# Begin of the value product in a product-key expert layer: order of row gathers, cell gathers and prepared activations, and the dense spill in two tensors

## The chip, the cores and the metric

The kernel runs on one core of one Trainium2 chip. The metric is the device time of one launch in microseconds (us). Three runs of the kernel before gave 3905.82, 3908.99 and 3909.05 us, median 3908.99 us.

## The reference

A decoder trunk of two layers, one sequence of 512 tokens, width 1024, all in float32. The part that this change touches is the retrieval of experts:

```
def peer_ffn(xn, w_query, sub_keys, expert_u, expert_v):
    q = einsum('bsd,dn->bsn', xn, w_query).reshape(b, s, 8, 2, 128)
    scores = einsum('bshpc,hpkc->bshpk', q, sub_keys)
    half_vals, half_idx = top_k(scores, 16)
    ...                                    # 256 sums per head, top 16 of them
    gates = softmax(top_vals)              # 8 heads x 16 = 128 slots per token
    u = take(expert_u, i_t)                # 16384 experts
    act = gelu(einsum('ted,td->te', u, x_t)) * g_t
    return einsum('te,ted->td', act, take(expert_v, i_t))
```

Before it in each layer stand the input projection, stick-breaking attention, a short convolution, a pooling mixer, gates and an output projection; behind it a gated embedding of the layer (`w_ple_gate`, `w_ple_proj`).

## The kernel before, in words

The host lays all weights out as one stream of tiles of 128 x 1024 float32 (512 KB), and the kernel works through them one by one. Each tile goes the same way: the SP queue loads it into one of 4 `raw` buffers (line 328), ScalarE rounds it to `hi` (`split`, line 453), VectorE or GpSimd takes the rest `lo = raw - hi` (`split`, lines 775 and 401), and TensorE multiplies with three products, hi x high, hi x low and lo x high. There are 8 buffers of `hi` and `lo` (`RING`), and tiles are split four ahead of their use (`AHEAD`). A `raw` buffer is loaded again as soon as `lo` of its tile is taken.

**The dense stage (U).** All 16384 experts are 128 tiles of `expert_u`. `experts` multiplies each tile with all 512 tokens (24 matmuls of 512 columns, line 1218). ScalarE takes the gelu into `eo` (`dense_gelu`, line 604) and spills its row of 512 tokens to the DRAM tensor `early`, of shape 128 x 128 x 512, by one DMA on its own queue (line 607), 256 KB each. `early_out` counts these DMAs. Meanwhile the softmax gates of the first 384 tokens (`M`) are scattered into `gate_table`.

**The value stage (V).** It treats two kinds of tokens apart, side by side.

- The first 384 tokens (`M` = 3 blocks of 128) go through all 128 tiles of `expert_v`. Four tiles are a group (`EG` = 4, `NG` = 32 groups per layer). For a group, ScalarE fetches gates `gb` and activations `eb` (`fetch`, lines 652 and 655, 768 KB each), VectorE multiplies them into `af` (`gated`, line 1115), ScalarE rounds to `ah` (`high`, line 660), VectorE takes `al = af - ah` (`low`, line 1122). TensorE then runs `values` (line 1434): 4 tiles x 3 blocks x 3 products x 2 halves = 72 matmuls of 512 columns. It waits for `al_ready` at the start of the group and for `lo_split` ahead of each tile. The sums stay in six PSUM banks.
- The last 128 tokens are not multiplied densely. Each has 128 slots, a slot being one chosen expert. For slot q of all 128 tokens, GpSimd gathers one activation each, the *cells* (`cells(q)`, line 413, an indirect DMA into column q of `hval`), and one row of `expert_v` each, the *rows* (`rows(j)`, line 421, an indirect DMA of 512 KB into one of 4 buffers `vrow`). VectorE multiplies four columns of cells with their gates into `aval` (line 1132) and adds `vrow * aval` to `acc` (the *axpy*, line 1137).

VectorE does one `period` per group. Its order is fixed: `gated` of the next group, wait for the four cells of this group (`h_in`, two semaphores in turn), `aval`, then four times a wait for a row, an axpy and a `split`, with `low` of the next group behind the second split. So a VectorE that waits for cells holds back the splits and `low` behind them. `low` of group g + 1 stands in the period of group g.

GpSimd's order before is written out: it waits for the last spill, issues cells 0 to 3, and then in turn `rows(j)`, `cells(j + 4)`. `rows(j)` from j = 4 on waits until the axpy of row j - 4 is done:

```
for q in range(4):
    cells(q)
for j in range(SLOTS):
    rows(j)
    if j + 4 < SLOTS:
        cells(j + 4)
```

At the end of V the sums of the 384 tokens and `acc` are turned back and added to `hT`.

## Time and profile before

| | us |
|---|---|
| median of three runs | 3908.99 |
| time of the profiled execution | 3910.81 |
| its span (first to last instruction) | 3909.0 |
| PE busy, share of the span | 3828.8, 98% |
| DVE busy, share | 2878.5, 74% |
| POOL busy, share | 1474.3, 38% |
| ACT busy, share | 1450.8, 37% |
| mean DMA rate over the span | 189 GB/s |
| mean granted TensorE clock | 0.992 of full speed |

The engines are PE (TensorE matmuls), DVE (VectorE), ACT (ScalarE), POOL (GpSimd) and SP (the load queue). A row of the timeline gives start, duration, engine, line and operation, and in square brackets how long the engine had been idle and what ended that. A q behind an engine's name is its DMA queue: for it, busy is the time of issuing. The chain of waits is the one sequence of work that ended last. "issue" as a releaser means that the profile shows nothing waited for.

### The profile page before, as it was taken

Reading aid. Unit: us, or ns where it says so; the run is one execution under the profiler, and the core shown is the slowest. Engines: PE = TensorE matmul, PEld = TensorE weight load, DVE = VectorE, ACT = ScalarE, POOL = GpSimd, SP = SyncE. Lnnn points to the kernel's source line nnn. Section 1 sums busy time; section 2 is a strip of 40 time slices with the busy share of each in tenths; the row PEclk is TensorE's granted clock in tenths of the full one; section 3 lists DMA queues with packets and bytes.
Section 4 is the critical chain, followed back from the end, with each engine's and each line's share of the span. In section 5 each row is a group of like instructions: output and inputs, shape, how many; then the busy total and the mean of one; then the engine's idle time right before and its main releaser. Section 6 shows DMA issues by size and latency. Waiting matters only on the chain.

```text
span 3909.0 us, 53929 instructions
## 1 busy us (share of the span) xinstructions
PE 3828.8 (98%) x17258; PEld 3140.4 (80%) x17258; DVE 2878.5 (74%) x4061; ACT 1450.8 (37%) x1957; POOL 1474.3 (38%) x935
## 2 busy tenths in 40 slices
PE   8999999999999999999999999999999999999997
PEld 5777888888888878888767778888888887888886
DVE  6753658989997287788577536599899963888785
ACT  5533333333333333333444333333333333333334
POOL 1100003444444277666101000045444443777651
PEclk9999999999999999999999999999999999999998
DMA  3222223445554699999222223234455546999991
GB/s 114 70 86 97 92 92 123 144 172 189 187 188 175 209 357 360 358 352 342 102 69 77 85 93 101 88 131 145 172 194 192 189 165 231 370 361 352 351 330 70
DMA packets 323770, 740.36 MB, mean 189 GB/s; under 512 B 30497, under 2 KB 161697, under 8 KB 319905
## 3 DMA queue, kind: packets, MB, share of 16 engines
q1 hardware_dynamic: 104400, 381.73, 28.1%
q10 hardware_dynamic: 174160, 222.40, 16.6%
q0 software_dynamic: 45056, 134.38, 9.3%
q8 instruction: 72, 1.18, 0.1%
q14 instruction: 82, 0.66, 0.1%
HBM read 618.87 MB, written 119.54 MB: 189 GB/s over the span
## 4 chain that ended last, share of the span: by engine, by line
PE 95%; DVE 2%; issue 1%; ACT 1%; DMA 1%; POOL 0%; DVEq 0%; ACTq 0%; POOLq 0%; SPq 0%
PE banks L1218 62%; PE banks L1434 26%; PE banks L1413 2%; PE banks L1280 1%; PE banks L1270 1%; PE banks L1288 1%; PE banks L1360 0%; ACT hi L453 0%; PE banks L1265 0%; DVE xl L787 0%; DMA vrow<-in_stream,tail_v 0%; DVE lo L775 0%; DMA raw<-in_stream 0%; ACT xh L469 0%; DVE xl L956 0%
## 5 line engine op out<-in xcount | busy, mean ns | idle before, releaser
L1218 PE MATMUL banks<-xh,hi 128*128 128x512 f32 x3264 | 1293.1, 396 | 27.1 <-DVE xl L787 18.5
L1218 PE MATMUL banks<-xl,hi 128*128 128x512 f32 x3264 | 1276.0, 391 | 0.0
L1218 PE MATMUL banks<-xh,lo 128*128 128x512 f32 x3264 | 1273.7, 390 | 0.0
L401 POOL TENSOR_TENSOR lo<-raw,hi 128x1024 fp32r<-128x1024 f32 x240 | 646.0, 2692 | 984.0 <-ACT hi L453 983.8
L775 DVE TENSOR_TENSOR lo<-raw,hi 128x1024 fp32r<-128x1024 f32 x484 | 586.6, 1212 | 418.2 <-ACT hi L453 351.7
L453 ACT ACTIVATE hi<-raw 128x1024 fp32r<-128x1024 f32 x724 | 739.5, 1042 | 261.3 <-DMA raw<-in_stream 162.6
L1218 PEld LDWEIGHTS banks<-xh,hi 128*128 128x128 f32 x3264 | 615.4, 189 | 166.0 <-DVE xl L787 23.6
L1218 PEld LDWEIGHTS banks<-xh,lo 128*128 128x128 f32 x3264 | 614.6, 188 | 130.9
L1218 PEld LDWEIGHTS banks<-xl,hi 128*128 128x128 f32 x3264 | 616.0, 189 | 122.4 <-issue 5.6
L1434 PE MATMUL banks<-hi,ah 128*128 128x512 f32 x1536 | 475.2, 391 | 13.2 <-issue 11.7
L1434 PE MATMUL banks<-lo,ah 128*128 128x512 f32 x1536 | 474.4, 390 | 0.0
L1434 PE MATMUL banks<-hi,al 128*128 128x512 f32 x1536 | 473.8, 390 | 0.0
L604 ACT ACTIVATE eo<-banks 128x512 f32<-128x512 f32 x256 | 153.3, 599 | 838.5 <-PE banks L1218 815.7
L413 POOL DMA_INDIRECT hval<-early,tail_h x256 | 395.7, 1546 | 167.1 <-DMA early<-eo 86.2
L1072 DVE TENSOR_TENSOR LB<-found,gates 128x1024 fp32r<-128x1024 f32 x192 | 414.1, 2157 | 0.1
L421 POOL DMA_INDIRECT vrow<-in_stream,tail_v x256 | 318.8, 1245 | 216.9 <-DVE acc L1137 145.7
L1137 DVE SCALAR_TENSOR_TENSOR acc<-vrow,aval,acc 128x1024 f32<-128x1024 f32 x256 | 330.5, 1291 | 43.5 <-DMA vrow<-in_stream,tail_v 24.2
L1434 PEld LDWEIGHTS banks<-hi,ah 128*128 128x128 f32 x1536 | 289.0, 188 | 74.8 <-issue 14.9
L1434 PEld LDWEIGHTS banks<-lo,ah 128*128 128x128 f32 x1536 | 289.4, 188 | 60.3
L1434 PEld LDWEIGHTS banks<-hi,al 128*128 128x128 f32 x1536 | 289.1, 188 | 60.3
L1066 DVE TENSOR_TENSOR found<-iota,tabs 128x1024 fp32r<-128x1024 f32 x192 | 233.6, 1217 | 42.7 <-PE banks L1413 42.7
L660 ACT ACTIVATE ah<-af 128x1536 fp32r<-128x1536 f32 x64 | 95.4, 1491 | 430.9 <-issue 209.7
(211 smaller groups left out, 3442.0 us busy)
## 6 DMA issues: line engine op xcount, KB each, us to landing
raw<-in_stream SPq DMA_DIRECT2D x724, 512.0 KB
early<-eo ACTq DMA_DIRECT2D x256, 256.0 KB, 2.4
gate_table<-stage ACTq DMA_DIRECT2D x24, 2048.0 KB, 7.1
gb<-gate_table ACTq DMA_DIRECT2D x64, 768.0 KB
eb<-early ACTq DMA_DIRECT2D x64, 768.0 KB
hval<-early,tail_h POOLq DMA_INDIRECT x256
vrow<-in_stream,tail_v POOLq DMA_INDIRECT x256
hT<-in_xT ACTq DMA_DIRECT2D x2, 1024.0 KB, 8.1
```

The lines of the kernel that those rows point to most:

```text
L401: pool.tensor_tensor(lo[k % RING][:, :], raw[k % RAW][:, :], hi[k % RING][:, :].bitcast(f32), ALU.subtract).then_inc(lo_split, 1)
L413: pool.indirect_dma_start(hval[:, q:q + 1], None, early_cells, bass.IndirectOffsetOnAxis(tail_h[:, q:q + 1], 0)).then_inc(h_in[q // 4 % 2] ...
L421: pool.indirect_dma_start(vrow[j % 4][:, :], None, stream_rows, bass.IndirectOffsetOnAxis(tail_v[:, j:j + 1], 0)).then_inc(vrow_in[j % 4], 16)
L453: act.activation(hi[k % RING][:, 0:w], raw[k % RAW][:, 0:w], ACT.Copy).then_inc(hi_split, 1)
L604: act.activation(eo[:, k % 2, :], bank[4 + k % 2][:, :], ACT.Gelu_apprx_tanh).then_inc(act_evac, 1)
L660: act.activation(ah[:, u, :, :], af[:, :, :], ACT.Copy).then_inc(ah_ready, 1)
L775: dve.tensor_tensor(lo[k % RING][:, 0:w], raw[k % RAW][:, 0:w], hi[k % RING][:, 0:w].bitcast(f32), ALU.subtract).then_inc(lo_split, 1)
L1066: dve.tensor_tensor(found[:, u, :, :, :], iota[:, :].unsqueeze(1).unsqueeze(1).to_broadcast(two), tabs[:, 0:2, cut].unsqueeze(3).to_broadc ...
L1072: dve.tensor_tensor(LB[:, u, :, :, :], found[:, u, 0, :, :].bitcast(f32).unsqueeze(2).to_broadcast(four), gates[:, :, cut].bitcast(f32).re ...
L1137: dve.scalar_tensor_tensor(acc[:, :], vrow[r][:, :], aval[:, z, r:r + 1], acc[:, :], ALU.mult, ALU.add).then_inc(axpy_done, 1)
L1218: ins = pe.matmul(out_ap, st[slot][:, a:a + P], mv, start=first and i == 0, stop=last and i == 2)
L1434: ins = pe.matmul(bank[m * 2 + h][:, :], a[:, z, k, m * P:(m + 1) * P], w[s % RING][:, h * SEQ:(h + 1) * SEQ], start=first and k == 0 and ...
```

## The change

Four edits.

1. GpSimd issues rows 0 to 3 first, ahead of the wait for the last spill and of all cells. Then cells 0 to 3, and from then on `cells(j)`, `rows(j)` with the same j.
2. VectorE's first two periods of V are written out of the loop. The first (`opens`) does `gated(1)`, the first split, `low(1)` and `gated(2)` and only then waits for the cells; no split stands behind its first axpy. The second (`taken`) leaves out its `gated`. The loop over the rest has one trip fewer. `Steps.loop` gets a start.
3. The dense spill goes to two tensors: `early`, now 128 x 128 x 384, for the first 384 tokens, and `late`, 128 x 128 x 128, for the others. That is two DMAs per tile in place of one (192 and 64 KB), and the counts of `early_out` are doubled.
4. `eb` is fetched from `early` without gaps: 4 x 384 values in one piece for each partition. The cells are gathered from `late`, with the indices worked out for it.

```diff
     @contextmanager
-    def loop(self, trips, per):
+    def loop(self, trips, per, start=0):
         base, k = self.base, self.k
-        with self.eng.Fori(0, trips) as i:
-            self.base, self.k = i * per + (base + k), 0
+        with self.eng.Fori(start, start + trips) as i:
+            self.base, self.k = i * per + (base + k - start * per), 0
...
-    early = nc.dram_tensor("early", (P, NK, SEQ), f32, kind="Internal").ap()
-    early_cells = early.rearrange("p e (t o) -> (p e t) o", o=1)
+    early = nc.dram_tensor("early", (P, NK, M), f32, kind="Internal").ap()
+    late = nc.dram_tensor("late", (P, NK, P), f32, kind="Internal").ap()
+    late_cells = late.rearrange("p e (t o) -> (p e t) o", o=1)
...
                 pool.wait_ge(tail_ready, l + 1)
                 pool.wait_ge(tile_done, RING + l * T + N_V)
+                for j in range(4):
+                    rows(j)
                 for u in range(2):
-                    pool.wait_ge(early_out[u], 16 + (l + 1) * (NK * 8))
+                    pool.wait_ge(early_out[u], 32 + (l + 1) * (NK * 16))
                 for q in range(4):
                     cells(q)
-                for j in range(SLOTS):
+                for j in range(4, SLOTS):
+                    cells(j)
                     rows(j)
-                    if j + 4 < SLOTS:
-                        cells(j + 4)
...
-                    act.dma_start(early[:, bass.ds(row, 1), :].rearrange("p a t -> p (a t)"), eo[:, k % 2, :])\
+                    act.dma_start(early[:, bass.ds(row, 1), :].rearrange("p a t -> p (a t)"), eo[:, k % 2, 0:M])\
+                       .then_inc(early_out[k % 2], 16)
+                    act.dma_start(late[:, bass.ds(row, 1), :].rearrange("p a t -> p (a t)"), eo[:, k % 2, M:SEQ])\
                        .then_inc(early_out[k % 2], 16)
...
-                    act.dma_start(eb[:, u, :, :], early[:, bass.ds(g * EG, EG), 0:M]).then_inc(early_in[u], 16)
+                    act.dma_start(eb[:, u, :, :], early[:, bass.ds(g * EG, EG), :]).then_inc(early_in[u], 16)
...
-                def period(i, z, prep=True):
+                def begin(g, u, turn):
+                    dve.wait_ge(al_ready, l * NG + g)
+                    gated(g, u, turn)
+                def period(i, z, prep=True, opens=False, taken=False):
                     k0 = N_V + z * EG + AHEAD
-                    if prep:
-                        dve.wait_ge(al_ready, l * NG + i * 2 + z + 1)
-                        gated(i * 2 + z + 1, 1 - z, i + (1 + z))
+                    g = i * 2 + z + 1
+                    if prep and not taken:
+                        begin(g, 1 - z, i + (1 + z))
+                    if opens:
+                        split(l, k0, i)
+                        low(g, 1 - z)
+                        begin(g + 1, z, i + (1 + z))
                     dve.wait_ge(h_in[z], l * (SLOTS * 8) + i * 64 + 64)
...
-                        split(l, k0 + r, i)
-                        if prep and r == 1:
-                            low(i * 2 + z + 1, 1 - z)
+                        if not opens or r > 0:
+                            split(l, k0 + r, i)
+                        if prep and r == 1 and not opens:
+                            low(g, 1 - z)
...
-                with steps.loop(NG // 2 - 1, DVE_TURN) as i:
+                period(0, 0, opens=True)
+                period(0, 1, taken=True)
+                with steps.loop(NG // 2 - 2, DVE_TURN, 1) as i:
                     period(i, 0)
                     period(i, 1)
```

GpSimd at the begin of V, before. `hval` are the cells, `vrow` the rows.

```order
L413 DMA hval<-early,tail_h 128x1 [waits early_out0,early_out1]
L413 DMA hval<-early,tail_h 128x1 x3
L421 DMA vrow_178<-in_stream,tail_v 128x1024
L413 DMA hval<-early,tail_h 128x1
L421 DMA vrow_179<-in_stream,tail_v 128x1024
L413 DMA hval<-early,tail_h 128x1
L421 DMA vrow_180<-in_stream,tail_v 128x1024
L413 DMA hval<-early,tail_h 128x1
L421 DMA vrow_181<-in_stream,tail_v 128x1024
L413 DMA hval<-early,tail_h 128x1
L419 ISA
L421 DMA vrow_178<-in_stream,tail_v 128x1024 [waits axpy_done]
```

Eight cells stand ahead of the first row that waits for an axpy (row 4): the cells of groups 0 and 1.

The same place after the change:

```order
L422 DMA vrow_179<-in_stream,tail_v 128x1024
L422 DMA vrow_180<-in_stream,tail_v 128x1024
L422 DMA vrow_181<-in_stream,tail_v 128x1024
L430 ISA
L414 DMA hval<-late,tail_h 128x1 [waits early_out0,early_out1]
L414 DMA hval<-late,tail_h 128x1 x4
L420 ISA
L422 DMA vrow_178<-in_stream,tail_v 128x1024 [waits axpy_done]
L414 DMA hval<-late,tail_h 128x1
L420 REGISTER_ALU
L422 DMA vrow_179<-in_stream,tail_v 128x1024 [waits axpy_done]
L414 DMA hval<-late,tail_h 128x1
```

Rows 0 to 3 have moved to the front, and five cells stand ahead of the first waiting row; cells 5, 6 and 7 now stand behind rows 4, 5 and 6, each of which waits for an axpy. In the rest of V the last cell of each group of four stands in the same way behind the third row of that group.

VectorE at the begin of V after the change (before, `aval` came directly behind the first `af`):

```order
L1119 TENSOR_TENSOR af<-eb,gb 128x1536
L778 REGISTER_ALU
L779 TENSOR_TENSOR lo_73<-raw_61,hi_65 128x1024
L1125 REGISTER_ALU
L1126 TENSOR_TENSOR al<-af,ah 128x1536
L1119 TENSOR_TENSOR af<-eb,gb 128x1536
L1144 ISA
L1145 TENSOR_TENSOR aval<-hval,tail_g 128x4
```

A split, `low(1)` and `gated(2)` have moved ahead of `aval`, which is the first instruction that needs cells.

## Rows read from the trace of the kernel before

**Rows 1.** Page, part 1: busy us (share of the span) and instructions by engine.

```profile
PE 3828.8 (98%) x17258; PEld 3140.4 (80%) x17258; DVE 2878.5 (74%) x4061; ACT 1450.8 (37%) x1957; POOL 1474.3 (38%) x935
```

**Rows 2.** What PE waited for: us in total, times, longest.

```profile
PE banks L1434 <- issue: 11.7, 2, 6.2
```

**Rows 3.** Timeline of PE at V's begin, both layers (start, us, what).

```profile
1353.13 0.72 PE L1434 MATMUL banks<-hi,ah 128*128 128x512 f32 x2 [0.76 <-ACT eo L604]
...
1369.14 0.61 PE L1434 MATMUL banks<-hi,al 128*128 128x512 f32 x2
1375.24 1.22 PE L1434 MATMUL banks<-hi,ah 128*128 128x512 f32 x2 [5.49 <-issue]
...
1380.18 0.62 PE L1434 MATMUL banks<-hi,ah 128*128 128x512 f32 x2
...
3314.41 1.22 PE L1434 MATMUL banks<-hi,ah 128*128 128x512 f32 x2 [6.23 <-issue]
...
3318.71 0.62 PE L1434 MATMUL banks<-hi,al 128*128 128x512 f32 x2
```

**Rows 4.** Chain of waits, in order of time: start, us, what.

```profile
1375.24 508.33 PE banks L1434 x2232
```

**Rows 5.** Timeline of POOL at V's begin.

```profile
1356.03 1.15 POOL L413 DMA_INDIRECT hval<-early,tail_h  x1 [43.13 <-DMA early<-eo]
...
1361.05 0.94 POOL L413 DMA_INDIRECT hval<-early,tail_h  x1 [0.31 <-issue]
1362.29 0.94 POOL L421 DMA_INDIRECT vrow<-in_stream,tail_v  x1 [0.30 <-issue]
```

**Rows 6.** Timeline of DVE at V's begin.

```profile
1356.91 1.76 DVE L1115 TENSOR_TENSOR af<-eb,gb 128x1536 f32<-128x1536 f32 x1 [0.64 <-DVE acc L1153]
1367.03 0.16 DVE L1132 TENSOR_TENSOR aval<-hval,tail_g 128x4 f32 x1 [8.36 <-DMA hval<-early,tail_h]
1368.64 1.28 DVE L1137 SCALAR_TENSOR_TENSOR acc<-vrow,aval,acc 128x1024 f32<-128x1024 f32 x1 [1.45 <-DMA vrow<-in_stream,tail_v]
```

**Rows 7.** Timeline of DVE in the second period of V: cells, `low`, the last axpy.

```profile
1381.46 0.15 DVE L1132 TENSOR_TENSOR aval<-hval,tail_g 128x4 f32 x1
...
1386.54 1.75 DVE L1122 TENSOR_TENSOR al<-af,ah 128x1536 fp32r<-128x1536 f32 x1
...
1393.10 1.32 DVE L1137 SCALAR_TENSOR_TENSOR acc<-vrow,aval,acc 128x1024 f32<-128x1024 f32 x1 [2.43 <-DMA vrow<-in_stream,tail_v]
```

**Rows 8.** Timeline of POOL beside it: rows 7 and 10, then a cell.

```profile
1382.66 1.27 POOL L421 DMA_INDIRECT vrow<-in_stream,tail_v  x1 [0.31 <-issue]
...
1391.91 0.94 POOL L421 DMA_INDIRECT vrow<-in_stream,tail_v  x1 [0.30 <-issue]
1393.16 0.94 POOL L413 DMA_INDIRECT hval<-early,tail_h  x1 [0.31 <-issue]
```

**Rows 9.** Timeline of POOL in the middle of V: a cell behind a waiting row.

```profile
1618.92 3.72 POOL L413 DMA_INDIRECT hval<-early,tail_h  x1 [0.30 <-issue]
```

**Rows 10.** Stretches: PE, PEld, DVE, ACT, POOL busy, PEclk, DMA share, GB/s.

```profile
1360.00:1368.00 8.00, 8.00 (x37) 6.60 (x36) 0.16 (x1) 3.14 (x4) 6.17 (x7) 1.00 0.99 306
1400.00:1860.00 460.00, 460.00 (x2031) 380.91 (x2030) 371.19 (x316) 157.50 (x145) 318.71 (x227) 1.00 0.99 354
```

**Rows 11.** DMA queues (packets, MB, share of 16 engines), and the spill's issues.

```profile
q1 hardware_dynamic: 104400, 381.73, 28.1%
q10 hardware_dynamic: 174160, 222.40, 16.6%
...
early<-eo ACTq DMA_DIRECT2D x256, 256.0 KB, 2.4
```

**Rows 12.** Timeline of ACT: the last gelu of the first layer's dense stage.

```profile
1352.40 0.60 ACT L604 ACTIVATE eo<-banks 128x512 f32<-128x512 f32 x1 [3.81 <-PE banks L1218]
...
1353.03 0.34 ACTq L607 DMA_DIRECT2D early<-eo  x1
```

**Rows 13.** Timeline of DVE: the last axpy of the first layer.

```profile
1868.35 1.28 DVE L1137 SCALAR_TENSOR_TENSOR acc<-vrow,aval,acc 128x1024 f32<-128x1024 f32 x1
```

14 lines of the change are left out of this document (7 added, 7 removed).

## The prediction, made before the change had run

> **What bounds the kernel now.** I read the busy shares first: TensorE is at 98% of the span, and the next engine, VectorE, at 74% [rows 1]. So only what TensorE waits for is worth anything, and the second view is that list. In the value stage it has one kind of entry, 11.7 us in two waits [rows 2], one for each layer. The third view is its place. TensorE starts group 0 of V at 1353.13; the last pair of matmuls of that group starts at 1369.14, a pair takes 0.45 us, and the next one starts only at 1375.24 [rows 3]. That is 5.65 us of standing still. Then TensorE runs at half speed: the six pairs up to 1380.18 take 4.94 us, where 2.72 would do, 2.2 us more. So the begin of V costs 7.9 us in the first layer, and 6.4 + 2.0 = 8.4 us in the second (idle 6.23 us, then five pairs in 4.30 us) [rows 3]. From there TensorE runs 2232 matmuls, which is 31 groups, in 508.33 us without a wait [rows 4]; less the 2.2 us that is **16.33 us for a group**.
>
> Why it stood: VectorE waited 8.36 us for the first four cells, until 1367.03 [rows 6], and `low(1)` and the splits for group 1 stand behind that wait. The cells were late because GpSimd could issue them only from 1356.03, when the last spill had landed [rows 5]; the fourth was issued by 1361.99 and landed, with VectorE's start, at 1367.03. So **a cell takes 5.04 us from the end of its issue to its use**.
>
> **The change, part by part.**
>
> *The begin.* `gated(1)`, the first split, `low(1)` and `gated(2)` now stand ahead of the wait for cells. `gated(1)` ended at 1358.67 before [rows 6]; with one split and one `low` behind it `al` of group 1 is there by about 1362, well ahead of 1369.6. GpSimd issues its four rows from about 1352.5, when the dense stage has ended, then cells 0 to 3. Four cells took 5.96 us before, and an issue repeats every 1.25 us at best [rows 5], so four rows end by 1358.5, four cells by 1363.5, and the cells are used at 1363.5 + 5.04 = 1368.5. Two axpys and a split later, about 4.0 us, the second tile of group 1 is split at 1372.6; TensorE wants it at 1369.6 + 4.1 = 1373.7. **The wait at group 1 goes: 7.9 and 8.4 us, 16.3 us in all.**
>
> *The order of the cells.* What is late next is the last cell of each later group. Before, eight cells stood ahead of the first row that waits; a cell was always issued four slots ahead of its own row. Now cell 4p + 3 is issued behind row 4p + 2, which waits for the axpy of row 4p - 2. This axpy is the third of the period before, and VectorE has only a split, an axpy, a split and `gated` between it and the wait for that cell. This makes a ring: cells used, three axpys, two splits and `low`, row issued, cell issued, cell landed, cells used. I price it from the second period, where VectorE ran from `aval` to the third axpy without a pause. `aval` is at 1381.46, `low` ends at 1388.29, the row behind the third axpy is issued at 1391.91 and the cell behind it by 1394.10 [rows 7, 8]. That is 12.64 us, and with the landing 12.64 + 5.04 = **17.68 us a group**, over the 16.33 that TensorE needs. From then on TensorE waits for `low` in every group.
>
> The landing is the unknown, since no row shows a cell that is waited for in the middle of V. From below: the spill, a DMA of another queue, lands 2.4 us after issue [rows 11]. From above: row 7 was issued by 1383.93 and used only at 1393.10 after a wait of 2.43 us, 9.17 us [rows 7, 8], with the DMA engines full. I take 5.04, the only row that shows the operation itself; it was measured with a DMA share of 0.99, and V now runs at 0.99 and 354 GB/s [rows 10]. At 17.68 us a group the same bytes would make 327 GB/s, close to the 306 beside those cells.
>
> For this landing a rule stands against the row. The Trainium skill, page "DMA: Bandwidth & Descriptors", section on the anatomy of one DMA, gives a DMA issued by GpSimd about 2.0 us and its bytes on top, so some 2 us for a cell. By it a group would take 14.6 us, below TensorE's 16.33, and nothing would be lost. The same page, section on queues, rings and completion order, says that a completion is written only after every earlier write of that DMA engine, across its queues. By that a cell ends no earlier than the rows and loads ahead of it, and the 5.04 us agree.
>
> *The sum, first layer.* Before cells 4 to 7 are complete, GpSimd issues row 4 (0.8 us behind the first axpy, at 1370.9), cell 5, row 5, cell 6, row 6 and cell 7, six issues at 1.25 us, to about 1378.1. They are used at 1383.1, and `low(2)` ends 6.83 us later at 1389.9, where TensorE wanted it at 1385.9: the wait has moved by one group. 29 further groups of 17.68 us lead to `low(31)` at 1902.7, and one group of matmuls to 1919.0. Before, V ended at 1375.24 + 508.33 = 1883.6 [rows 4]. That is 35.4 us more, already with the begin's gain in it; the second layer, whose begin gave 0.5 us more away, 34.9. Together 70.3 us: 3981.1 for the profiled execution's 3910.8, and since the median of the runs lies 1.8 us below that, **3979 us**.
>
> *The spill in two pieces.* 256 more issues on ScalarE's queue at 0.34 us [rows 12] are 87 us of issuing, at nothing: ScalarE is idle for 3.8 us of each tile [rows 12]. Without that cover they would be the 87 us. The pieces land 2.4 us after issue and are wanted again two tiles later, 48 matmuls of 0.227 us or 10.9 us. At V's begin the second piece lands some 0.4 us later than the one before did, behind GpSimd's four rows. Nothing.
>
> *`eb` without gaps.* The ACT queue, with the small pieces, took 16.6% for 222 MB, the load queue, with pieces of 4 KB, 28.1% for 382 MB [rows 11]: 0.075 and 0.074% for a MB. So larger pieces give the DMA engines next to nothing back; between 0 and perhaps 0.2 us of a landing. The trip written out of VectorE's loop adds instructions that are fetched once: nothing, up to a us a layer.
>
> *The end of V.* The last axpy ended at 1869.63 [rows 13], 14 us ahead of TensorE. In the ring that lead shrinks to about a us behind `low(31)` plus one group; the turning back waits for it only after 2.7 us of other matmuls. Nothing, at most 2 us a layer.
>
> **The rivals.**
>
> *The cell lands soon enough (faster).* The point from which it decides is a landing of 3.69 us, where the ring is as long as TensorE's group. For it: the rule above; the spill's 2.4 us; and that GpSimd's pace in the priced period was partly its own backlog, so that the ring may be a us or so shorter. Against it: 5.04, measured, and rows at over 5 us. With a landing of 2.4 us, cells 4 to 7 are used at 1380.5, `low(2)` ends 1.4 us late, and the rest runs at 16.33: 6.4 and 7.0 us gained, 3910.8 - 13.4, for the median **3896 us**. If even this 1.4 us is hidden, 3893. Chance 0.27.
>
> *The ring is as long as TensorE's group.* Break even is where 29 groups give back the begin, a group of 16.47 us: 3909 us. Chance 0.06.
>
> *The ring is longer still.* For it: the cell behind a waiting row took 3.72 us to issue in the middle of V [rows 9], 2.8 more than the one I priced. With one cell in three like that, a group takes 18.6 us and the kernel about 4033 us; with all of them 20.5 and about 4140; with the row's 9.17 us of landing 21.8 and about 4230. Against it: as a group gets longer the DMA engines have less to do. I count it within the slower case, which has 0.67; a tenth lies beyond 4055.
>
> *The begin gains nothing.* If the rows ahead make the first cells land later than 1369.5, TensorE waits at the second tile of group 1. It would cost up to what was saved, 16 us, and changes no sign; it lies within the range of the slower case.
>
> **How the numbers follow.** A measurement of this kernel tells about 0.2%, 8 us, from no change. Slower 0.67, the same 0.06, faster 0.27. In the slower case alone the time goes from 3927 us (a cell lands together with the row ahead of it: the first row took 5.4 us from 1363.23 to its axpy at 1368.64 [rows 5, 6], less 1.25 us, a group of 16.8) to 4055 (18.9 a group). The range must reach the faster case, so 3892 to 4055.
>
> **What would show it.** In the trace of the changed kernel: no wait of TensorE at group 1; TensorE waiting in V not once but at nearly every group, by 1 to 1.5 us each; VectorE's `aval` with a wait for cells of 2 us or more in each period; a distance of 17 to 18.5 us from `aval` to `aval`; V longer by 35 us a layer; GpSimd's cells evenly behind its rows. I am wrong if `aval` waits for less than a us in the middle of V and TensorE runs without gaps there. Then the landing was the term that failed, and V is about 6 to 8 us shorter a layer.

## The result, and the profile after

| | us |
|---|---|
| before, median of 6 runs | 3909.88 (3905.82 to 3911.20) |
| after, median of 6 runs | 4182.64 (4156.32 to 4192.57) |
| ratio, 95% interval | 1.0685 (1.0648 to 1.0722) |
| profiled execution after: time, span | 4156.32, 4154.5 |
| mean granted TensorE clock, before and after | 0.992, 0.969 |

The change makes the kernel 273 us slower. The forecast said slower, 3979 us, with a range to 4055: the sign came, the size did not. Where the runs of one program below lie more than 1.5% apart, the ratio is that of the faster ones alone.

The page of the kernel after, parts 1, 4 and 5. A group's row gives busy us and mean ns of one, then the idle time before it and what ended most of it.

```profile
PE 3913.9 (94%) x17258; PEld 3188.2 (77%) x17258; DVE 2858.3 (69%) x4061; ACT 1466.9 (35%) x1957; POOL 1532.7 (37%) x935
...
PE 65%; issue 15%; DMA 11%; DVE 4%; POOL 4%; ACT 1%; DVEq 0%; POOLq 0%; ACTq 0%; SPq 0%
...
L414 POOL DMA_INDIRECT hval<-late,tail_h x256 | 376.0, 1469 | 78.0 <-issue 78.0
...
L1145 DVE TENSOR_TENSOR aval<-hval,tail_g 128x4 f32 (+1 forms) x64 | 10.4, 163 | 451.3 <-DMA hval<-late,tail_h 451.3
```

What PE waited for, after: us in total, times, longest.

```profile
PE banks L1450 <- DVE al L1126: 159.8, 45, 6.9
...
PE banks L1234 <- DVE lo L779: 9.3, 2, 5.7
...
PE banks L1450 <- DVE lo L779: 1.9, 2, 1.1
```

(L1234 with `lo` is the first multiplication behind V; the other two are in V.) Where V knew two waits of 11.7 us in all [rows 2], TensorE now waits 45 times for `al`, 159.8 us. The cells have come into the chain that ended last (`hval`, in the 11% of DMA), and VectorE stands 451.3 us for them in 64 periods. The account closes: the waits above make 171.0 us, 159.3 more than the 11.7 before. PE's busy time, for the same 17258 matmuls, went from 3828.8 [rows 1] to 3913.9, 85.1 more. Together that is 244.4 of the 245.5 us by which the span grew. The busy part is matmuls at half speed behind the waits. It is no loss of its own where VectorE sets the pace: there the slow matmuls only fill a part of the stop, as the groups below show.

**The begin of V.** Timeline of PE, first layer:

```profile
1375.55 0.73 PE L1450 MATMUL banks<-hi,ah 128*128 128x512 f32 x2 [1.05 <-DVE lo L779]
...
1394.29 1.22 PE L1450 MATMUL banks<-hi,ah 128*128 128x512 f32 x2 [6.18 <-DVE al L1126]
```

Timeline of VectorE there:

```profile
1371.35 0.16 DVE L1145 TENSOR_TENSOR aval<-hval,tail_g 128x4 f32<-128x4 f32 x1 [7.28 <-DMA hval<-late,tail_h]
...
1387.26 0.16 DVE L1145 TENSOR_TENSOR aval<-hval,tail_g 128x4 f32<-128x4 f32 x1 [7.00 <-DMA hval<-late,tail_h]
...
1392.35 1.74 DVE L1126 TENSOR_TENSOR al<-af,ah 128x1536 fp32r<-128x1536 f32 x1
```

Timeline of POOL there:

```profile
1354.00 1.14 POOL L422 DMA_INDIRECT vrow<-in_stream,tail_v  x1 [40.44 <-PE banks L1234]
...
1361.33 1.76 POOL L414 DMA_INDIRECT hval<-late,tail_h  x1 [0.30 <-issue]
1363.40 1.49 POOL L414 DMA_INDIRECT hval<-late,tail_h  x1 [0.31 <-issue]
...
1373.85 1.32 POOL L422 DMA_INDIRECT vrow<-in_stream,tail_v  x1 [6.46 <-DVE acc L1150]
...
1381.50 0.95 POOL L414 DMA_INDIRECT hval<-late,tail_h  x1 [0.31 <-issue]
```

The wait at group 1 (5.49 us [rows 3]) is down to 1.05. At group 2 there is one of 6.18, and behind it the first pair takes 1.22 us, the half speed. The first cells are used at 1371.35; they had been priced at 1368.5. GpSimd began 1.5 us later than priced, and three of its issues took 1.5 to 1.8 us instead of 0.94.

**The middle of V** has two kinds of groups. The distance from `aval` to `aval` is about 17.8 us in one and about 21.7 in the other (medians). Over the first layer it is 20.30 on average (from 1371.35 to 2000.53 in 31 steps). A short one, VectorE:

```profile
1405.07 0.16 DVE L1145 TENSOR_TENSOR aval<-hval,tail_g 128x4 f32 x1 [4.54 <-DMA hval<-late,tail_h]
...
1410.55 1.75 DVE L1126 TENSOR_TENSOR al<-af,ah 128x1536 fp32r<-128x1536 f32 x1
...
1413.42 1.26 DVE L779 TENSOR_TENSOR lo<-raw,hi 128x1024 fp32r<-128x1024 f32 x1
1414.61 1.32 DVE L1150 SCALAR_TENSOR_TENSOR acc<-vrow,aval,acc 128x1024 f32<-128x1024 f32 x1
1415.85 1.21 DVE L779 TENSOR_TENSOR lo<-raw,hi 128x1024 fp32r<-128x1024 f32 x1
...
1423.29 0.16 DVE L1145 TENSOR_TENSOR aval<-hval,tail_g 128x4 f32 x1 [4.56 <-DMA hval<-late,tail_h]
```

The same, GpSimd: a row, the third cell of the four, the row behind it, and the last cell.

```profile
1411.76 1.36 POOL L422 DMA_INDIRECT vrow<-in_stream,tail_v  x1 [0.30 <-issue]
1413.43 0.94 POOL L414 DMA_INDIRECT hval<-late,tail_h  x1 [0.30 <-issue]
1414.67 0.95 POOL L422 DMA_INDIRECT vrow<-in_stream,tail_v  x1 [0.30 <-issue]
1415.93 1.96 POOL L414 DMA_INDIRECT hval<-late,tail_h  x1 [0.30 <-issue]
```

A long one, VectorE:

```profile
1713.89 0.17 DVE L1145 TENSOR_TENSOR aval<-hval,tail_g 128x4 f32 x1 [8.44 <-DMA hval<-late,tail_h]
...
1721.80 1.22 DVE L779 TENSOR_TENSOR lo<-raw,hi 128x1024 fp32r<-128x1024 f32 x1
1722.93 1.28 DVE L1150 SCALAR_TENSOR_TENSOR acc<-vrow,aval,acc 128x1024 f32<-128x1024 f32 x1
1724.13 1.22 DVE L779 TENSOR_TENSOR lo<-raw,hi 128x1024 fp32r<-128x1024 f32 x1
1725.26 1.75 DVE L1119 TENSOR_TENSOR af<-eb,gb 128x1536 f32<-128x1536 f32 x1
1735.48 0.16 DVE L1145 TENSOR_TENSOR aval<-hval,tail_g 128x4 f32 x1 [8.47 <-DMA hval<-late,tail_h]
```

The same, GpSimd:

```profile
1721.81 2.03 POOL L414 DMA_INDIRECT hval<-late,tail_h  x1 [0.30 <-issue]
1724.14 3.69 POOL L422 DMA_INDIRECT vrow<-in_stream,tail_v  x1 [0.31 <-issue]
1728.13 0.95 POOL L414 DMA_INDIRECT hval<-late,tail_h  x1 [0.30 <-issue]
```

And TensorE behind it:

```profile
1738.48 0.61 PE L1450 MATMUL banks<-hi,al 128*128 128x512 f32 x2
1742.59 1.22 PE L1450 MATMUL banks<-hi,ah 128*128 128x512 f32 x2 [3.49 <-DVE al L1126]
...
1745.91 0.63 PE L1450 MATMUL banks<-lo,ah 128*128 128x512 f32 x2
```

In both kinds the third cell meets the third split of the period, to a hundredth of a us. That is no chance: the row ahead of it is held by `low` and ends 0.82 us after `low` does (1411.76 + 1.36 = 1413.12, and 1410.55 + 1.75 = 1412.30), 0.30 us pass between two issues, and the third split begins 1.12 us behind `low` too (1413.42), with one axpy between them.

In the short group the cell starts 0.01 us behind the split, takes 0.94, and the row behind it finds only an axpy. In the long one it starts 0.01 us behind the split as well, yet takes 2.03: it ends at 1723.84, 0.82 us after the split's end (1723.02). Now the row begins level with the fourth split, which `gated` follows without a gap, and ends at 1727.83, again 0.82 us after the end of `gated` (1727.01). The last cell is issued 15.19 us after `aval` (1729.08 less 1713.89), in the short group 12.82 (1417.89 less 1405.07). It lands after 6.40 us instead of 5.40.

Of the 60 groups behind the first of each layer, the row took over 3 us in 34. In these the last cell was issued 15.3 us after `aval` on average and landed in 6.2, in the others 13.2 and 5.4. I call the third cell held when its issue takes over 1.9 us; of the 56 cells for which the trace has the cell and the split beside it, 36 were held.

TensorE follows: behind a stop of 3.49 us it goes at half speed, four pairs up to 1745.91 take 3.32 us where 1.81 would do. The 21.59 us of this group are TensorE's 16.33, these 1.5 and the stop of 3.5 (21.3). At full speed the stop would have been 1.5 us longer and the group as long.

### The profile page after: what moved, and what is told of

The parts are those of the page before. It is cut to its first block, busy times and chain, and to the rows that moved or that the text cites. A ratio compares the mean times of both kernels' runs of the same rounds, so it can differ in the third digit from the quotient of the medians.

```text
span 4154.5 us, 54167 instructions
## 1 busy us (share of the span) xinstructions
PE 3913.9 (94%) x17258; PEld 3188.2 (77%) x17258; DVE 2858.3 (69%) x4061; ACT 1466.9 (35%) x1957; POOL 1532.7 (37%) x935
## 3 DMA queue, kind: packets, MB, share of 16 engines
q10 hardware_dynamic: 186448, 222.42, 15.7%
## 4 chain that ended last, share of the span: by engine, by line
PE 65%; issue 15%; DMA 11%; DVE 4%; POOL 4%; ACT 1%; DVEq 0%; POOLq 0%; ACTq 0%; SPq 0%
PE banks L1234 59%; DMA hval<-late,tail_h 11%; POOL vrow L422 3%; DVE acc L1150 2%; PE banks L1429 2%; PE banks L1296 1%; PE banks L1286 1%; PE banks L1304 1%; POOL hval L414 1%; PE banks L1376 0%; ACT hi L455 0%; PE banks L1281 0%; DVE xl L791 0%; DVE aval L1145 0%; DVE lo L779 0%
## 5 line engine op out<-in xcount | busy, mean ns | idle before, releaser
L1234 PE MATMUL banks<-xh,hi 128*128 128x512 f32 x3264 | 1293.2, 396 | 27.9 <-DVE xl L791 19.3
L1234 PE MATMUL banks<-xl,hi 128*128 128x512 f32 x3264 | 1276.4, 391 | 0.0
L1234 PE MATMUL banks<-xh,lo 128*128 128x512 f32 x3264 | 1273.8, 390 | 0.0
L1234 PEld LDWEIGHTS banks<-xh,hi 128*128 128x128 f32 x3264 | 615.6, 189 | 166.5 <-DVE xl L791 24.4
L1234 PEld LDWEIGHTS banks<-xh,lo 128*128 128x128 f32 x3264 | 614.9, 188 | 130.8
L1234 PEld LDWEIGHTS banks<-xl,hi 128*128 128x128 f32 x3264 | 616.1, 189 | 122.8 <-issue 5.6
L1450 PE MATMUL banks<-hi,ah 128*128 128x512 f32 x1536 | 509.2, 414 | 163.4 <-DVE al L1126 159.8
L422 POOL DMA_INDIRECT vrow<-in_stream,tail_v x256 | 396.3, 1548 | 503.6 <-DVE acc L1150 352.9
L1450 PE MATMUL banks<-lo,ah 128*128 128x512 f32 x1536 | 497.7, 407 | 0.0
L1450 PE MATMUL banks<-hi,al 128*128 128x512 f32 x1536 | 495.0, 405 | 0.0
L1450 PEld LDWEIGHTS banks<-hi,ah 128*128 128x128 f32 x1536 | 303.4, 201 | 246.8 <-issue 182.3
L414 POOL DMA_INDIRECT hval<-late,tail_h x256 | 376.0, 1469 | 78.0 <-issue 78.0
L1076 DVE TENSOR_TENSOR LB<-found,gates 128x1024 fp32r<-128x1024 f32 x192 | 395.3, 2059 | 0.1
L1450 PEld LDWEIGHTS banks<-lo,ah 128*128 128x128 f32 x1536 | 305.3, 199 | 67.7
L1450 PEld LDWEIGHTS banks<-hi,al 128*128 128x128 f32 x1536 | 303.6, 198 | 66.7
L1145 DVE TENSOR_TENSOR aval<-hval,tail_g 128x4 f32 (+1 forms) x64 | 10.4, 163 | 451.3 <-DMA hval<-late,tail_h 451.3
## 6 DMA issues: line engine op xcount, KB each, us to landing
eb<-early ACTq DMA_DIRECT2D x64, 768.0 KB, 10.7
```

What stands on the lines that cost most here:

```text
L414: pool.indirect_dma_start(hval[:, q:q + 1], None, late_cells, bass.IndirectOffsetOnAxis(tail_h[:, q:q + 1], 0)).then_inc(h_in[q // 4 % 2], 16)
L422: pool.indirect_dma_start(vrow[j % 4][:, :], None, stream_rows, bass.IndirectOffsetOnAxis(tail_v[:, j:j + 1], 0)).then_inc(vrow_in[j % 4], 16)
L1076: dve.tensor_tensor(LB[:, u, :, :, :], found[:, u, 0, :, :].bitcast(f32).unsqueeze(2).to_broadcast(four), gates[:, :, cut].bitcast(f32).re ...
L1234: ins = pe.matmul(out_ap, st[slot][:, a:a + P], mv, start=first and i == 0, stop=last and i == 2)
L1450: ins = pe.matmul(bank[m * 2 + h][:, :], a[:, z, k, m * P:(m + 1) * P], w[s % RING][:, h * SEQ:(h + 1) * SEQ], start=first and k == 0 and ...
```

## The experiments

**e1, the spill alone.** Edits 3 and 4, in the kernel before:

```diff
-    early = nc.dram_tensor("early", (P, NK, SEQ), f32, kind="Internal").ap()
+    early = nc.dram_tensor("early", (P, NK, M), f32, kind="Internal").ap()
+    late = nc.dram_tensor("late", (P, NK, P), f32, kind="Internal").ap()
...
+                    act.dma_start(late[:, bass.ds(row, 1), :].rearrange("p a t -> p (a t)"), eo[:, k % 2, M:SEQ])\
```

> The kernel before with the spill alone changed: two DMAs per tile, `early` without gaps, cells gathered from `late`. Theory (a ring: the last cell of a group stands behind a row that waits for an axpy): the ring is not there, so 3909 us within 6 us, and no wait for cells in the middle of V. Rival (gathering from `late`, or the small pieces, makes a cell land later and that is what costs): 4100 us or more.

Measured: 3907.45 us (3906.21 to 3911.63), the kernel before beside it 3908.37; ratio 0.9998 (0.9989 to 1.0008), as expected. The 256 more issues and the pieces without gaps cost and give nothing.

**e2, GpSimd's order alone.** In the kernel before:

```diff
-                for j in range(SLOTS):
+                for j in range(4):
+                    rows(j)
+                for j in range(4, SLOTS):
+                    cells(j)
                     rows(j)
-                    if j + 4 < SLOTS:
-                        cells(j + 4)
```

(cells 0 to 3 stand ahead of all rows, as before.)

> The kernel before with GpSimd's order alone changed: cells 0 to 3 first as before, rows 0 to 3, then cells(j), rows(j). Theory of the ring: all of the loss and none of the begin's gain, so 4170 to 4210 us, and 18 to 22 us from aval to aval. Rival (the spill, or VectorE's new begin, is to blame): 3905 to 3915 us.

Measured: 4019.39 us (4009.62 to 4022.82); 1.0278 (1.0261 to 1.0295). What PE waited for in V:

```profile
PE banks L1435 <- DVE al L1123: 78.1, 47, 7.2
```

Here the ring is what the prediction had priced: 18.0 us a group on average in both layers, 12.97 and 12.84 from `aval` to the end of the last cell's issue, 5.03 and 5.12 from there to the next `aval`. Only 1 of 55 third cells was held. So the order costs 111 us, and the changed kernel loses 163 more by something that this program has not got. The expectation, written from the long groups, was wrong.

**e3, the lead of four given back** in the changed kernel (rows 0 to 3 still first):

```diff
-                for q in range(4):
+                for q in range(8):
                     cells(q)
                 for j in range(4, SLOTS):
-                    cells(j)
                     rows(j)
+                    if j + 4 < SLOTS:
+                        cells(j + 4)
```

> The changed kernel with only the cells' lead given back: cells 0 to 7, then rows(j), cells(j + 4). Theory of the ring: the loss of 270 us goes altogether, what is left is the gain at V's begin. That gain is 16.3 us less the waits that the changed kernel still shows at group 1 for the splits (9.3 us in two, with some half speed behind them): 3895 to 3905 us. Rival (spill or VectorE's begin cost): 4100 us or more.

Measured: 3900.43 us (3896.00 to 3905.90); 0.9979 (0.9969 to 0.9988). The whole loss is gone by the place of one kind of instruction: 282 us below the changed kernel, and 8 below the kernel before, which is what is left of the begin's gain. This is what had been expected.

**e4, VectorE's begin alone**, edit 2 in the kernel before:

```diff
-                    if prep:
-                        dve.wait_ge(al_ready, l * NG + i * 2 + z + 1)
-                        gated(i * 2 + z + 1, 1 - z, i + (1 + z))
+                    g = i * 2 + z + 1
+                    if prep and not taken:
+                        begin(g, 1 - z, i + (1 + z))
+                    if opens:
+                        split(l, k0, i)
+                        low(g, 1 - z)
+                        begin(g + 1, z, i + (1 + z))
...
```

> The kernel before with VectorE's begin alone changed: a split, low(1) and gated(2) ahead of the wait for cells; GpSimd's order as before. Theory: the cells are used at 1367.0 as before, the second axpy ends at about 1371.2 and the split behind it at 1372.4, ahead of TensorE's 1373.7, so the whole wait goes without any row ahead of the cells: 3892 to 3896 us. Rival (the rows must be ahead as well): TensorE waits at group 1 for the splits by 3 us or more a layer, 3900 to 3909 us.

Measured: 3905.40 us (3902.28 to 3909.95); 0.9992 (0.9982 to 1.0001). Timeline of PE:

```profile
1388.83 1.22 PE L1446 MATMUL banks<-hi,ah 128*128 128x512 f32 x2 [3.86 <-DVE al L1122]
```

The wait at group 1 is gone, and one of 3.86 us (3.76 in the second layer) stands at group 2, with slow matmuls behind it that cost 1.4 and 1.6 us. The first cells are used at 1366.30, about as before. What holds `low(2)` up is rows: ahead of it VectorE waits 2.18, 2.54, 1.26 and 1.06 us for them, and its second `aval` waits for nothing. The expectation of 3892 to 3896 us missed; the time is the rival's, but not by the rival's wait.

**e5 and e6: which edit makes the groups long.** e5 is e2 and e1 together, e6 the changed kernel without edits 3 and 4 (one tensor `early` again, the diff of e1 backwards). e5:

```diff
-                for j in range(SLOTS):
+                for j in range(4):
+                    rows(j)
+                for j in range(4, SLOTS):
+                    cells(j)
                     rows(j)
...
+    late = nc.dram_tensor("late", (P, NK, P), f32, kind="Internal").ap()
```

> The kernel before with GpSimd's order and the spill in two, without rows ahead and without VectorE's new begin. The order alone cost 111 us, the whole change 274. Theory S (the missing 163 us are the spill's, which costs nothing without the ring but lengthens the ring): 4170 to 4200 us, 20 us or more a group. Theory D (the missing part comes with rows ahead and VectorE's begin): 4010 to 4030 us, 17.9 us a group. Theory P (it is a matter of how GpSimd's issues fall against VectorE's tensor_tensor instructions, which hold them up; any shift may tip it): in between, with long and short groups in one run.

Measured: 4006.26 us (4002.19 to 4016.41); 1.0250 (1.0235 to 1.0266), 17.8 us a group, and of 56 third cells none was held. So theory S is out.

> The changed kernel with the spill as before (one DMA per tile, `early` for all tokens). Theory S: 4000 to 4030 us. Theory D: 4150 to 4200 us. Theory P: whichever, but the time goes by the number of groups in which the row ahead of the last cell takes 3.7 us to issue: some 4 us for each such group over 17.5 us.

Measured, four runs: 4083.49, 4102.18, 4182.72 and 4186.54 us; 1.0468 (1.0441 to 1.0494). In the profiled one, the longest, a group takes 20.8 and 20.5 us and 45 of 56 third cells are held. So the long groups do not need the spill. Against e5 two things are new, edit 2 and the four rows ahead of the first cells; which of them brings the long groups was not run. Neither changes anything inside the loops that run these groups. That the two shorter executions had fewer long groups was not seen, since only one was profiled; and as both lie below all six of the changed kernel, it is not shown either that the spill has no part in how many there are.

**e7, another form of the instruction.** In the changed kernel the splits and `low` of V's periods are written as one `scalar_tensor_tensor`, times 1.0, less `hi`, which is the axpy's form:

```diff
-                    dve.tensor_tensor(al[:, u, :, :], af[:, :, :], ah[:, u, :, :].bitcast(f32), ALU.subtract)\
+                    dve.scalar_tensor_tensor(al[:, u, :, :], af[:, :, :], 1.0, ah[:, u, :, :].bitcast(f32), ALU.mult, ALU.subtract)\
...
```

> The changed kernel with VectorE's splits and low in V's periods written as scalar_tensor_tensor (times 1.0, minus), which takes some 0.06 us more each and computes the same. Theory P (a tensor_tensor on VectorE holds up GpSimd's issue until 0.8 us behind its end, a scalar_tensor_tensor does not): hardly an issue over 2 us but beside gated, from aval to the end of the last cell's issue 11 to 12 us instead of 14.3, a group of about 17, 3970 to 4020 us. Rival (what holds GpSimd up is VectorE's work as such, or its own queue): nothing changes, 4150 to 4200 us.

Measured, four runs: 4066.00, 4172.41, 4198.29 and 4201.22 us. In the profiled execution (4201.22) 20.8 us a group, and issues of 2.03 and 3.69 us as before, 43 of 53 third cells held. The form is not what holds an issue up; theory P is wrong in this point.

**e8, no fetches from group 3 on**, in the changed kernel:

```diff
-                            fetch(i * 2 + z + 3, 0, 1 - z)
+                            act.sem_inc(gate_in[1 - z], 16)
+                            act.sem_inc(early_in[1 - z], 16)
```

> The changed kernel without the fetches of gates and activations from group 3 on, which leaves their 1.5 MB a group out (old contents are used). Theory (a cell lands late because bytes of other queues and the rows are ahead of it): from the end of the cell's issue to aval 4.5 us or less on the mean, where the changed kernel shows 5.8; 4080 to 4140 us. Rival (a gather's landing is a fixed time): 5.5 us or more, and the time within 1% of 4183 us.

Measured, two runs: 4007.85 and 4026.45 us; 1.0274 (1.0248 to 1.0301). Windows of 200 us in V: PE, PEld, DVE, ACT, POOL busy, PEclk, DMA share, GB/s. The changed kernel:

```profile
1700.00:1900.00 200.00, 173.63 (x694) 139.80 (x693) 121.91 (x104) 52.85 (x48) 121.41 (x77) 0.90 0.81 271
```

e8:

```profile
1700.00:1900.00 200.00, 188.78 (x800) 152.61 (x799) 143.81 (x123) 59.63 (x55) 139.43 (x89) 0.97 0.69 233
```

42 of 57 third cells are held, as in the changed kernel, and `aval` to the last issue is as long, 14.4 and 14.6 us. But the landing falls from 5.9 and 5.7 to 3.7 and 3.6 us, and a group from 20.3 and 19.9 to 18.1. The time fell further than expected. Most of it falls where the fetches are issued ahead of the last cell. In the long group above they start at 1727.19 and 1727.76, and the cell is issued by 1729.08; in the short one the cell is out by 1417.89, ahead of the fetches at 1418.91 and 1419.47. With the fetches gone the landing falls from 6.2 to 3.1 us in the groups with a long row, and only from 5.4 to 4.6 in the others. So on average 2.2 us of a landing, and 3.1 in a long group, belong to the fetches. The Trainium skill, page "DMA: Bandwidth & Descriptors", section on queues, rings and completion order, has a completion written only after every earlier write of that DMA engine; the runs are in line with it, 5.9 us with the fetches and 3.7 without, though they do not tell it from a shared rate.

**e9, a nudge.** In the changed kernel VectorE also clears one column, ahead of the third split:

```diff
+    nudge = sb("nudge", o_c + 3904, [P, 1])
...
+                        if r == 2:
+                            dve.memset(nudge[:, :], 0.0)
```

> The changed kernel with one tiny instruction more on VectorE in each period: a memset of one column ahead of the split behind the third axpy. In the traces so far GpSimd's issue of the sixth of eight (the cell behind row 4p + 5) and this split begin within 0.02 us of each other; where the issue is first or level it takes 0.94 us and the group 17.5, where it is 0.01 to 0.02 us late it takes 2.03, the row behind it 3.7 and the group 21.8. Theory (this tie decides): the added work lets GpSimd be first every time, no group over 20 us but a few at loop ends, and the kernel gets FASTER by some 170 us for doing more: 3990 to 4020 us. Rival (the long groups have another cause, as the rows ahead or the landing): 4150 to 4200 us as before.

Measured: 4009.34 us (4004.95 to 4011.36); 1.0255 (1.0241 to 1.0269). **An instruction more in each period, and the kernel is 173 us faster.** Timeline of VectorE:

```profile
1728.40 0.16 DVE L1146 TENSOR_TENSOR aval<-hval,tail_g 128x4 f32 x1 [4.48 <-DMA hval<-late,tail_h]
...
1736.43 1.25 DVE L780 TENSOR_TENSOR lo<-raw,hi 128x1024 fp32r<-128x1024 f32 x1
1736.45 0.06 DVE L1154 MEMSET nudge<- 128x1 f32 x1
...
1746.28 0.16 DVE L1146 TENSOR_TENSOR aval<-hval,tail_g 128x4 f32 x1 [4.55 <-DMA hval<-late,tail_h]
```

GpSimd:

```profile
1736.43 0.94 POOL L415 DMA_INDIRECT hval<-late,tail_h  x1 [0.30 <-issue]
1737.67 0.94 POOL L423 DMA_INDIRECT vrow<-in_stream,tail_v  x1 [0.30 <-issue]
1738.92 1.96 POOL L415 DMA_INDIRECT hval<-late,tail_h  x1 [0.30 <-issue]
```

TensorE, and the same window as above:

```profile
1735.44 0.73 PE L1453 MATMUL banks<-hi,ah 128*128 128x512 f32 x2 [1.14 <-DVE al L1127]
```

```profile
1700.00:1900.00 200.00, 189.23 (x814) 153.26 (x815) 148.59 (x139) 61.88 (x56) 122.12 (x92) 0.99 0.93 318
```

(The program has the memset ahead of the split, the profile 0.02 us behind its start: at this grain its order is not to be trusted.) Of 57 third cells none is held; 55 start level with the split or 0.01 us ahead, 2 start 0.01 us behind. A group takes 17.8 and 17.7 us, 12.5 and 5.2 in its two parts. TensorE stands 1.1 us instead of 3.5, starts at full speed, and the granted clock in this window is 0.99 instead of 0.90. The forecast from the tie came true in sign and size, with nothing else changed: the long groups hang on it.

**e10, a lead of two** in the changed kernel:

```diff
-                for q in range(4):
+                for q in range(6):
                     cells(q)
                 for j in range(4, SLOTS):
-                    cells(j)
                     rows(j)
+                    if j + 2 < SLOTS:
+                        cells(j + 2)
```

> The changed kernel with the cells two slots ahead of their rows in place of level (cells 0 to 5, then rows(j), cells(j + 2)). The last cell of a group then stands behind row 4p + 5, which the second axpy releases, not the third: issued some 3 to 5 us sooner in the ring. Theory: from aval to the end of the last cell's issue 9 to 10 us, a ring of 14 to 16 us, under TensorE's 16.33, so all of the loss goes: 3898 to 3912 us. Rival (the lead of four is needed, for a landing of 9 us as the rows show): 3930 us or more.

Measured: 3907.90 us (3903.12 to 3910.20); 0.9996 (0.9987 to 1.0006). The last cell is now issued 9.0 and 9.1 us after `aval`, and `aval` follows 6.7 and 6.6 us later: 15.7 us on average, below TensorE's 16.33. In 5 of the 31 steps of the first layer `aval` did not wait for cells at all, so not all of the 6.7 is landing. The loss ends there. Against e3, 7.5 us are missing; stops and slow matmuls at the begin make 9.0 us in both layers where e3 has 4.6. PE's waits in the first layer:

```profile
1375.48 0.74 PE L1451 MATMUL banks<-hi,ah 128*128 128x512 f32 x2 [1.56 <-DVE lo L780]
...
1390.54 0.72 PE L1451 MATMUL banks<-hi,ah 128*128 128x512 f32 x2 [2.49 <-DVE al L1127]
```

**e11 and e12: all four splits ahead of the first cells.** e11 is e3 with this, e12 is e4 with it (cells first):

```diff
+                        for r in range(1, 4):
+                            split(l, k0 + r, i)
...
-                        if not opens or r > 0:
+                        if not opens:
                             split(l, k0 + r, i)
```

> Candidate for the best version: the kernel with the cells' lead of four given back, and in VectorE's first period all four splits ahead of the wait for cells. The kernel with the lead alone (3900.4 us) still showed waits of 2.4 and 0.8 us at group 1 for the splits and 1.0 and 0.3 at group 3. Theory: the first pair goes, with the half speed behind it: 3893 to 3898 us. Rival (the splits free raw buffers, their four loads lie ahead of the cells in the DMA engines, and low(2) comes late instead): 3900 to 3910 us with a wait of TensorE at group 2.

Measured: 3900.70 us (3898.35 to 3904.22); 0.9979 (0.9970 to 0.9988). Timeline of PE:

```profile
1388.18 0.72 PE L1453 MATMUL banks<-hi,ah 128*128 128x512 f32 x2 [2.45 <-DVE al L1127]
```

> The other candidate: the kernel before, with GpSimd's order and spill untouched, and VectorE's new begin with all four splits ahead of the wait. With the begin alone (3905.4 us) TensorE waited 3.9 and 3.8 us at group 2, since low(2) stood behind axpys that waited for rows and a split that waited for its load. Theory: the loads start sooner, so the second cause goes and the first stays: 3895 to 3903 us. Rival: no change, 3903 to 3908 us.

Measured: 3905.19 us (3902.63 to 3910.76); 0.9993 (0.9984 to 1.0002). Timeline of PE:

```profile
1389.71 0.73 PE L1448 MATMUL banks<-hi,ah 128*128 128x512 f32 x2 [3.44 <-DVE al L1122]
1390.27 0.99 PE L1448 MATMUL banks<-lo,ah 128*128 128x512 f32 x2
```

In both the wait at group 1 is gone altogether and comes back one group later, and neither gains on what it was made from (3900.43 and 3905.40): both theories missed, and it went as the two rivals said. With the rows first the stops at group 2 are 2.45 and 2.70 us, and there is one of 1.53 later on; cells first, they are 3.44 and 3.54. Slow matmuls behind them cost 1.6 us in the first layer of e11 and none in the second, and 1.5 and 1.6 in e12. That is 8.3 against 10.1 us, 1.8 of the 4.5 us between the medians. The rest is not explained, and the two profiled executions lie only 1.2 us apart.

**e13, the tie moved from the other side.** In e5, GpSimd gets one semaphore instruction more ahead of the third cell of each group of four, the one that meets the split.

```diff
+                    if q >= 4 and q % 4 == 2:
+                        apart(pool)
```

> The kernel of e5 (order and spill, 4006 us, all groups short) with one semaphore instruction more on GpSimd ahead of the cell that begins level with VectorE's split. Theory (who is first in the tie decides): GpSimd now comes second, that cell takes 2.03 us to issue and the row behind it 3.7 in nearly every group, 20 to 22 us a group, 4150 to 4220 us. Rival (the tie is not enough, the long groups need the rows ahead or VectorE's begin): 4000 to 4020 us.

Measured: 4006.23 us (4000.28 to 4012.42); 1.0245 (1.0229 to 1.0260). This tells nothing: the instruction vanished in the 0.30 us that lie between two issues anyway, and the third cells start as they did in e5: all 56 are free, 55 of them level with the split or 0.01 us ahead. The tie was not moved.

**e14, `low(2)` ahead of the second wait too**, on top of e11:

```diff
+                    if taken:
+                        split(l, k0, i)
+                        low(g, 1 - z)
...
-                        if not opens:
+                        if not opens and not (taken and r == 0):
                             split(l, k0 + r, i)
-                        if prep and r == 1 and not opens:
+                        if prep and r == 1 and not opens and not taken:
```

> The kernel of e11 (3900.7 us) with VectorE's second period changed as well: the first split and low(2) ahead of its wait for cells and rows. In e11 low(2) stood behind two axpys, the first of which waited 4.9 us for its row, and TensorE waited 2.5 and 2.7 us for it at group 2. Theory: these waits go, 5 us and the slower matmuls behind them: 3892 to 3897 us, all of the begin's 16 us but for a remainder. Rival (the lag of VectorE only moves on, to group 3): 3898 to 3903 us.

Measured: 3897.16 us (3893.92 to 3904.76), the kernel before beside it 3907.91; 0.9973 (0.9961 to 0.9985). What PE waited for `al` in V, both layers:

```profile
PE banks L1456 <- DVE al L1127: 0.9, 2, 0.7
```

The begin of V is free of waits but for these 0.9 us and the 0.76 at each start that the kernel before has too [rows 3]. This is the fastest version of the study, at the upper end of what was expected, 10.7 us below the kernel before and 285 below the changed one. The begin had been priced at 16.3 us; where the rest stays is not shown.

## Why the prediction was right, and where it failed

**Right: the sign, and the mechanism behind it.** The last cell of each group behind a row that waits makes a ring longer than TensorE's group. Its price, 12.64 + 5.04 = 17.68 us, came out at 18.0 in e2, 17.8 in e5 and 17.8 and 17.7 in e9. e3 and e10 show that nothing else in the change costs time. That 12.64 hits the 12.5 of e9 is partly luck. In the priced period the row started 10.45 us after `aval`, behind GpSimd's backlog, and the last cell took 0.94 us [rows 7, 8]. In e9's period above the row starts at 9.27, and the cell takes 1.96, held by the fourth split: two errors of about a us against each other.

**Right: the spill** (e1, 0.9998). **Right: the wait at group 1 goes and comes back at group 2**, though not in size: 1.05 us were left at group 1, and the second wait was 6.18 us where 4.0 had been priced. Row 4 and the cells behind it came 4.2 us later than the sum had it (`aval` at 1387.26 for 1383.1): 2.9 of them by the first cells, the rest by issues of 1.32 and 1.97 us where the sum went by 0.94 (one in 1.25 us with the pause).

**Right: the rule for a short landing, weighed and left.** "Some 2 us for a cell" would have left nothing to lose. The landings were 5.0 to 5.9 us in V, and 3.6 with the fetches gone.

**Wrong: the term of 12.64 us, and the tenth given to the rival "the ring is longer still".** From `aval` to the end of the last cell's issue the changed kernel took 14.4 us on average in the first layer and 14.2 in the second, not 12.64, and the landing was 5.9 and 5.7, not 5.04: 20.3 and 19.9 us a group for 17.68. The sum had taken the issues as they fell in one period, row and last cell free at 0.94 us each, and left out that VectorE's own instructions hold them up. The rival had the very row that decides, a cell with 3.72 us of issue [rows 9], and was priced "with one cell in three like that". In the changed kernel 34 of 60 groups had it, in the row ahead of the last cell. Such a group cost more than the issue: 2.4 us of issuing and 1.0 of landing between the two groups shown, 21.7 us instead of 17.8 in the median. Between e9, without them, and the changed kernel lie 173 of the 273 us. The argument "as a group gets longer the DMA engines have less to do" held for the rate (271 GB/s for 318) and did not help: in a long group the last cell is issued behind the group's own fetches, in a short one ahead of them (e8).

**Wrong in size: what the short ring costs.** e9, the priced ring, stands at 4009 us, 30 above the forecast. V's first layer ended at 1927.8 in it where the sum had 1919.0, mostly by the later group 2. "The end of V: nothing, at most 2 us a layer" was 3.6 and 3.8 us in e9, and 5.74 and 3.54 in the changed kernel: `aval` of the last group waits for its cells (until 2000.53), four axpys and three splits stand behind it, and the projection's first split comes after them.

**Neither right nor wrong: the clock.** The forecast went by the ring and left out what stops do to TensorE's speed. Where the ring sets the pace that is sound (above). It costs time behind a single stop, with a TensorE-bound stretch after it: 2.2 and 2.0 us at the begin of V in the kernel before [rows 3], 1.4 to 1.6 us a layer in e4 and e12, and 1.6 in one of e11's two layers.

**What stays open.** In e6 and in the changed kernel the tie falls against GpSimd, in e5 for it, though the loops have the same instructions. What differs ahead of them is edit 2 and the four rows first, and no run has one without the other beside this order. In the programs with short groups the cell starts level with the split or 0.01 us ahead (51 of 55 in e2), in the changed kernel level to 0.02 us behind (all 56). This much is measured; where the 0.01 us comes from is not. A cell that starts 0.01 us behind was held in 27 cases of 38 in the changed kernel, so the profile's grain is too coarse to tell who was first. That the tie alone would make e5 long was not shown, since e13 did not move it.

## What to carry to other kernels

When an order is changed so that a gather stands behind something that waits for the consumer, price the ring (use, release, issue, landing, use) and hold it against the bound engine's period; a lead of two slots made 17.7 us into 15.7, and the whole loss vanished. An engine whose issue ends a fixed time after another engine's instruction can meet that engine's next instruction to a hundredth of a us, in every round. If two engines in such a ring start instructions at the same moment, the worse outcome deserves as much of the forecast as the better one, above all where the trace of before already shows an instance of it. And move preparation ahead of a wait for every group whose work stands behind it, or the wait moves one group on (e4, e11, e12) and goes only when that one is prepared as well (e14).

## What the runs showed of the hardware

**An indirect DMA's issue on GpSimd is held by VectorE's split, `low` and `gated`.** Free, it takes 0.94 us; held by one of them it ended 0.82 us after that instruction's end (1723.84 for 1723.02, 1727.83 for 1727.01, 1413.12 for 1412.30). Whether it is held through two of them back to back hangs on its start. In the traces of the changed kernel, e2, e6 and e9, all 88 issues that start level with a split that `gated` follows, or up to 0.02 us behind it, took 3.68 to 3.71 us; all 142 that start 0.03 to 0.15 us behind it took 1.95 to 1.98, as the last cell at 1415.93 did, 0.08 us behind its split. Why is not shown. An axpy of the same width, with `vrow` and `acc` as inputs, did not hold it: the row issued at 1414.67, 0.95 us, lies within the axpy of 1414.61 (1.32 us). e7 shows that it is not the instruction's form; what sets the axpy apart stays open. The Trainium skill, page "SBUF — State Buffer", section on who interferes with whom, has a VectorE instruction with two SBUF inputs contend with a GpSimd instruction that reads SBUF, but infers that `tensor_tensor` does not stall the writing of descriptors. The runs here differ from that: 0.94 us became 2.03 and 3.69 beside `tensor_tensor`, so the measurement decides.

**The clock behind a stop.** In the changed kernel the granted clock was 0.50 of full speed from 1742.60 to 1745.30 us, right behind the stop of 3.49 us, and 1.00 from 1746 on; 0.50 is the lower of the two levels, 1.2 GHz. After stops of 3.49, 3.86 and 6.18 us TensorE's first pair took 1.22 us; after 1.05, 1.14, 2.45 and 2.49 us it took 0.72 to 0.74. A quick first pair does not mean that nothing is lost. In e11's first layer the slow pairs begin 1.0 us behind the end of the 2.45 us stop; in e12 the first pair behind 3.44 us took 0.73 and the one behind it 0.99. Nor does the length of the stop decide alone. After 3.37 us the changed kernel has a first pair of 1.22 us (at 1787.08) and one of 0.72 (at 3750.80), with no slow pair in the 2 us behind the second. In the window 1700 to 1900 us the granted clock was 0.90 of full speed with the long groups and 0.99 with the short ones.
